# Two projections as seven block products each, and the last norm along token rows

## The reference, cut to what matters

```python
# S5 mixer: h is 512 tokens x 1024, w_in is 1024 x 4096, u takes the first 2048 columns
u_l, g_l = jnp.split(h_lat @ w_in, 2, axis=-1)
u_c, g_c = jnp.split(h_ctx @ w_in, 2, axis=-1)
...
# end of the second block: 256 tokens, 2816 -> 1024
h = h + (jax.nn.silu(gate) * val) @ w_down
return rmsnorm(h, final_norm_g)      # h * rsqrt(mean(h*h) + eps) * g, along the 1024
```

## Time and profile before

| what | value |
|---|---|
| median of 3 runs | 1619.56 us (1618.23 to 1621.71) |
| the profiled execution | 1622.5 us |
| its span, first to last instruction | 1620.7 us |
| mean granted TensorE clock | 0.979 of full speed |
| TensorE busy | 1512.4 us, 93% of the span |
| VectorE, ScalarE, GpSimd busy | 850.1, 388.6, 492.7 us |

### The profile page before, as it was taken

One profiled execution on the slowest core, in us unless ns is written; L12 is line 12 of the kernel. 1 busy time (PEld: TensorE's weight loads), 2 busy tenths in 40 slices (PEclk: granted clock), 3 DMA queues, 4 the chain that ended last, 5 costly groups with the idle time before them and its releaser, 6 DMA issues.

```text
span 1620.7 us, 25958 instructions
## 1 busy us (share of the span) xinstructions
PE 1512.4 (93%) x10248; PEld 1145.9 (71%) x10248; DVE 850.1 (52%) x1538; ACT 388.6 (24%) x889; POOL 492.7 (30%) x478
## 2 busy tenths in 40 slices
PE   5999989998999889998777999999999899999898
PEld 3444556665644478877666788888887788888787
DVE  6769265676569853367658665542441233433201
ACT  1133333333300031245444210000211011233201
POOL 0159999999894069221111000000000000000000
PEclk9999999999999999999998999999999999999999
DMA  9598787778798636669998725342443333444341
GB/s 395 161 280 270 197 209 190 185 208 199 182 276 293 251 78 189 272 213 331 324 313 258 302 107 207 142 170 105 155 146 114 105 129 108 152 155 155 123 143 72
DMA packets 70932, 318.76 MB, mean 197 GB/s; under 512 B 15536, under 2 KB 19760, under 8 KB 46256
## 3 DMA queue, kind: packets, MB, share of 16 engines
q1 hardware_dynamic: 36608, 222.84, 38.5%
q0 software_dynamic: 26672, 67.55, 17.1%
q10 hardware_dynamic: 7552, 26.96, 4.5%
HBM read 267.08 MB, written 50.20 MB: 196 GB/s over the span
## 4 chain that ended last, share of the span: by engine, by line
PE 42%; DMA 10%; DVE 1%; POOL 1%; issue 1%; ACT 1%; SPq 0%; ACTq 0%; POOLq 0%; DVEq 0%
PE bank L873 27%; PE bank L1192 10%; DMA s_responses<-arena 8%; PE bank L1310 2%; DMA arena<-in_glu 1%; POOL arena L2790 1%; DMA arena<-s_responses 1%; PE bank L1368 0%; PE bank L1355 0%; PE bank L1334 0%; DVE arena L2328 0%; PE bank L1299 0%; PE bank L1201 0%; PE bank L1147 0%; PE bank L1262 0%
## 5 line engine op out<-in xcount | busy, mean ns | idle before, releaser
L873 PE MATMUL bank<-arena,ring 128*128 128x256 f32 x1312 | 287.1, 381 | 4.4 <-DVE arena L2637 4.4
L873 PEld LDWEIGHTS bank<-arena,ring 128*128 128x128 f32 x1312 | 251.0, 191 | 39.5 <-DVE arena L2637 4.8
L873 PE MATMUL bank<-gate,ring 128*128 128x256 f32 (+1 forms) x640 | 196.7, 470 | 5.4 <-DVE gate L2532 3.4
L873 PEld LDWEIGHTS bank<-gate,ring 128*128 128x128 f32 x640 | 123.4, 193 | 78.1 <-issue 62.2
L873 PE MATMUL bank<-ht,ring 128*128 128x256 f32 (+1 forms) x544 | 175.1, 481 | 0.1
L873 PEld LDWEIGHTS bank<-ht,ring 128*128 128x128 f32 x544 | 102.5, 190 | 69.8 <-issue 60.6
L1192 PE MATMUL bank<-arena 128*128 128x256 f32 x576 | 127.3, 379 | 2.8 <-DVE pw L2372 2.5
L1192 PEld LDWEIGHTS bank<-arena 128*128 128x128 f32 x576 | 108.7, 190 | 17.9 <-issue 2.8
L1068 PE MATMUL bank<-ring,ht 128*128 128x256 f32 x512 | 114.3, 385 | 6.5 <-DVE ht L1927 6.5
L1068 PEld LDWEIGHTS bank<-ring,ht 128*128 128x128 f32 x512 | 98.4, 193 | 20.4 <-issue 6.8
L2265 DVE COPY arena<-bank 64x256 f32<-64x256 f32 x64 | 27.0, 422 | 81.8 <-PE bank L1079 80.0
(11 more groups left out here) (423 smaller groups left out, 2497.4 us busy)
## 6 DMA issues: line engine op xcount, KB each, us to landing
ring<-in_w_up SPq DMA_DIRECT2D x22, 1024.0 KB, 4.7
ring<-in_mod_tail SPq DMA_DIRECT2D x16, 1024.0 KB, 6.7
arena<-s_b_powers SPq DMA_DIRECT2D x16, 1024.0 KB, 9.4
ring<-in_glu SPq DMA_DIRECT2D x16, 1024.0 KB, 8.2
arena<-in_glu SPq DMA_DIRECT2D x16, 1024.0 KB, 9.0
arena<-s_b_rows POOLq DMA_DIRECT2D x24, 512.0 KB, 10.6
arena<-s_power_rows POOLq DMA_DIRECT2D x24, 512.0 KB, 11.4
s_b_powers<-arena POOLq DMA_DIRECT2D x24, 512.0 KB, 4.7
```

The source lines that it names most:

```text
L873: mm = pe.matmul(psum[2 * (u % 2) + m][:, 0:mv.free_size()], ring[:, sl, k, m * P:(m + 1) * P], mv, start=(kg == 0 and k == 0), stop=(kg = ...
```

## The change

```diff
-            sp.wait_ge(bm_stored, 32 * 2)
-            for b in range(2):
-                load_bm(b)
             sp.wait_ge(bm_stored, 32 * N_POOL)
             sp.wait_ge(cp_stored, 32 * N_POOL)
-            for b in range(3):
-                load_cp(b)
+            load_cp(0)
+            load_cp(2)
+            sp.wait_ge(prod_read, u_step(2, "c21"))
+            load_cp(1)
             for s in range(2):
                 load_gate(s)
+            sp.wait_ge(prod_done, u_product(3, "p6"))
+            load_bm(0)
+            sp.wait_ge(prod_done, u_product(3, "p7"))
+            load_bm(1)
+            sp.wait_ge(bbd_set, 1)
+            load_b(2)
...
-            stream("w_down", 3, 4, last=KF - 16)
...
+            sp.wait_ge(o2_done, XH)
+            for j in range(2):
+                load_down(0, j)
...
+            for j in range(2, 4):
+                load_down(0, j)
+            sp.dma_start(gain_row, a["final_norm_g_2"].partition_broadcast(P)).then_inc(x_in, 16)
+            sp.wait_ge(prod_done, down_product(0, "p1"))
+            for j in range(2):
+                load_down(1, j)
+            sp.wait_ge(sums_set, down_sum("t1"))
+            load_down(1, 2)
+            sp.wait_ge(prod_done, down_product(0, "p3"))
+            sp.wait_ge(sums_set, down_sum("t2"))
+            load_down(1, 3)
...
-                        mm = pe.matmul(psum[2 * (u % 2) + 1 - s4 // 2][:, (1 - s4 % 2) * S:(2 - s4 % 2) * S],
-                                       ht[:, k, s4 * P:(s4 + 1) * P], ring[:, sl, k, :], start=(k == 0), stop=(k == KD - 1))
-                mm.then_inc(slot_done, 1)
...
+            def u_block(c, name, bank, lhs, rhs, first=True, last=True, ready=None):
...
+                        mm = pe.matmul(psum[bank][:, (1 - t) * S:(2 - t) * S], lhs[:, k, t * P:(t + 1) * P], rhs[:, k, :],
+                                       start=(first and t == 0 and k == 0), stop=(last and k == 3), skip_group_check=True)
+                mm.then_inc(prod_done, 1)
...
+                b11, t1, b21, b22 = u_blocks(c)
...
+                    u_block(c, "p1", 0, ht[:, 0:4, lat_1], b11, ready=turned_in)
+                    u_block(c, "p2", 3, ht[:, 4:8, lat_1], b21, ready=lambda k: turned_in(4 + k))
...
+                    u_block(c, "p1", 0, ht[:, 0:4, lat_1], b11, last=False)
+                    pe.wait_ge(prod_done, u_product(c - 1, "p4"))
+                    pe.sem_inc(slot_done, 2)
...
+                pe.wait_ge(sums_set, max(u_sum("s1"), u_sum("t1", c)))
+                u_block(c, "p5", 1, s1, t1, last=False)
+                pe.wait_ge(sums_set, max(u_sum("s2"), u_sum("t2", c)))
+                if c:
+                    pe.wait_ge(prod_read, u_step(c - 1, "u3"))
+                u_block(c, "p6", 2, s2, u_t24, last=False)
+                pe.wait_ge(*u_loaded(c, 1))
+                pe.wait_ge(sums_set, u_sum("s4"))
+                pe.wait_ge(utok_set, u_copy(c, "s5"))
+                u_block(c, "p3", 1, s4, b22, first=False)
+                pe.wait_ge(sums_set, max(u_sum("s3"), u_sum("t3", c)))
+                pe.wait_ge(prod_read, u_step(c, "s2"))
+                u_block(c, "p7", 2, s3, u_t3, first=False)
+                if c == 3:
+                    responses(0)
+                if c:
+                    pe.wait_ge(utok_set, u_copy(c, "s1"))
+                    u_block(c, "p2", 0, ht[:, 4:8, lat_1], b21, first=False)
+                if c == 3:
+                    responses(1)
+                u_columns(2 * c)
+                pe.wait_ge(sums_set, u_sum("t4", c))
+                pe.wait_ge(prod_read, u_step(0, "c11") if c == 0 else u_step(c - 1, "c21"))
+                u_block(c, "p4", 3, ht[:, 4:8, lat_2], u_t24)
...
+            pe.sem_inc(slot_done, 2)
+            u_columns(7)
             pe.sem_inc(yt_set, 1)
             for q in range(2):
                 pe.wait_ge(unit_free[q], unit_at["s5_out"])
             gate_rows(0)
...
-            pe.wait_ge(ff_set, KF + 2)
-            linear("w_down", 3, 4, lambda k: ff[:, k, :], last=KF - 16)
-            for f in range(2):
-                pe.wait_ge(xn_set, 3 * KD + 4 * (f + 1))
-                for t in range(2):
-                    for j in range(4):
-                        mm = pe.transpose(psum[4 + 2 * t + f][:, j * P:(j + 1) * P], xn[:, 4 * f + j, t * P:(t + 1) * P], ident)
-                    mm.then_inc(t2_done, 1)
...
+            for h in range(2):
+                for k in range(KD):
+                    mm = pe.transpose(psum[4 + 2 * h + k // 4][:, k % 4 * P:(k % 4 + 1) * P], xl[:, k, h * P:(h + 1) * P], ident)
+                mm.then_inc(t2_done, 1)
...
+                    if ready:
+                        pe.wait_ge(ff_set, ready + k)
+                    mm = pe.matmul(psum[bank][:, 0:MT2], lhs[:, k, :], rhs(k), start=(first and k == 0), stop=(last and k == KH - 1),
...
+                if c == 0:
+                    for m in range(4):
+                        pe.wait_ge(unit_free[m // 2], unit_at["end"])
+                    down_block(0, f11, b11, ready=3)
+                    pe.wait_ge(down_in[1], 32)
+                    down_block(3, f12, b21, ready=3 + KH)
...
+                pe.wait_ge(sums_set, max(down_sum("s1"), down_sum("t1", c)))
+                down_block(1, s1, t1, last=False)
+                pe.wait_ge(sums_set, max(down_sum("s2"), down_sum("t2", c)))
...
+                down_block(2, s2, t24, last=False)
...
+                pe.wait_ge(sums_set, down_sum("t4", c))
+                pe.wait_ge(prod_read, down_step(0, "c11") if c == 0 else down_step(0, "c21"))
+                down_block(3, f22, t24)
...
+                act.wait_ge(prod_done, u_product(c, "p1"))
+                if c == 3:
+                    act.wait_ge(bm_stored, 32 * N_POOL)
+                    act.wait_ge(cp_stored, 32 * N_POOL)
+                elif c:
+                    act.wait_ge(prod_read, u_step(c - 1, "c21"))
+                act.copy(s1, psum[0][:, :]).then_inc(utok_set, 1)
+                act.wait_ge(prod_done, u_product(c, "p5"))
+                if c:
+                    act.wait_ge(prod_read, u_step(c - 1, "c22"))
+                act.copy(u_s5, psum[1][:, :]).then_inc(utok_set, 1)
...
+            for h in range(2):
+                act.wait_ge(t2_done, NB5 + 1 + h)
+                for z in range(2):
+                    act.copy(x_tok[:, h, z * 512:(z + 1) * 512], psum[4 + 2 * h + z][:, :]).then_inc(xr_set, 1)
...
+                    act.wait_ge(sq_done, 3 * KD + 2)
+                    square(0, 0, 1024, 0)
+                    act.wait_ge(sq_done, 3 * KD + 3)
+                    act.activation(r_tok[:, 0:1], row_ms[:, 0, 0:1], ACT.Sqrt, bias=eps, scale=1.0 / D).then_inc(root_set, 1)
...
+                    act.wait_ge(prod_read, down_step(1, "c21"))
+                    square(1, 512, 768, 2)
+                    act.wait_ge(sq_done, 3 * KD + 4)
+                    act.wait_ge(kv2_set, 16 + 2)
+                    act.activation(r_tok[:, 1:2], row_ms[:, 1, 2:3], ACT.Sqrt, bias=row_ms[:, 1, 0:1], scale=1.0 / D).then_inc(root_set, 1)
+                    act.wait_ge(root_set, 15)
+                    act.activation(orow[:, 1, 0:512], orow[:, 1, 0:512], ACT.Copy, scale=r_tok[:, 1:2]).then_inc(av_set, 1)
...
+            def operand(o, x, y, op, needs=0):
...
+                tt(o, x, y, op).then_inc(sums_set, 1)
...
+            u_t3_t1(0)
+            u_t2(0)
             dve.wait_ge(mod_set, 5)
...
+                else:
+                    u_columns(2 * c - 1)
+                dve.wait_ge(prod_done, u_product(c, "p6"))
+                dve.wait_ge(utok_set, u_copy(c, "s1"))
+                if c:
+                    dve.wait_ge(prod_read, u_step(c - 1, "c12"))
+                u_read(t2_, bank[2], t1_, ALU.add)
+                u_t4(c)
+                if c == 0:
+                    for k in range(4, KD):
...
+                u_read(of_unit(0, 1), by_group(bank[1]), by_group(t2_), ALU.add, u_step(c, "s2"))
...
+                u_read(t1_, bank[2], t1_, ALU.add)
...
+                u_read(of_unit(0, 0), by_group(t1_), by_group(u_s5), ALU.add, u_step(c, "u3"))
+                if c < 3:
+                    u_t3_t1(c + 1)
+                u_columns(2 * c)
+                dve.wait_ge(prod_done, u_product(c, "p4"))
...
+                u_read(of_unit(1, 0), by_group(t1_), by_group(bank[3]), ALU.subtract)
+                if c < 3:
+                    u_t2(c + 1)
+                if c < 2:
+                    for b in (2 * c, 2 * c + 1):
+                        angles(N_TURN + b)
+            u_columns(7)
...
-            add_out("w_down", 3, 3, "final_norm_g_2")
...
+            down_t3_t1(0)
+            dve.wait_ge(ff_set, KF + 2)
+            row_operand(s1, f21, f22, ALU.add)
+            row_operand(s2, s1, f11, ALU.subtract, (down_sum("s1"),))
+            down_t2(0)
+            row_operand(s4, f12, s2, ALU.subtract, (down_sum("s2"),))
+            row_operand(s3, f11, f21, ALU.subtract)
...
```

(10 more changed lines are left out.)

493 lines of the change are left out of this document (358 added, 135 removed).

## The result

The changed kernel takes 1613.23 us (median of 17 runs, 1607.41 to 1623.09) against 1621.71 us for the kernel before (17 runs, 1614.32 to 1638.17): ratio 0.995, 95% interval 0.9931 to 0.997. It is faster, by 8 us of the 23.5 that were forecast, and the time lies above the range of 1589 to 1605. The profiled execution took 1616.82 us, its span is 1615.0.

What follows compares the result with a forecast made beforehand. TensorE, busy 93% of the span, was taken to bound the kernel outside a transfer-paced loop. S5's -7 us at `inputs(0)` and the end's -16.5 us gave 1619.6 - 23.5 = 1596 us, range 1589 to 1605.

Steps and rivals of the forecast that it cites:

- The end: Last projection and final norm: start, products, waits and tail together were to give -16.5 us.
- The start: Last projection: turning the residual at once lets its first product start at 1530.6 instead of 1532.52, -1.9 us.
- The products: Last projection: 154 products at full clock take 66.5 us against 78.4 before, -11.9 us.
- The wait ahead of p5: Last projection: TensorE waits for VectorE's sums before p5, +1.5 us.
- The tail: From the last product to the end of the span: 5.5 us instead of 9.7, -4.2 us.
- The loop and all behind it: Recurrence's loop of response stores behind the S5 part: paced by transfers, carried over unchanged.
- S5, products: S5 projection: 256 block products become 224 at 0.432 us each, -13.8 us.
- S5, start: S5 projection: three sums of weights in VectorE's row before the first reciprocal delay the first product, +2.4 us.
- S5, the price of a row beside GpSimd: S5 projection: a VectorE sum of 1024 pays 1.07 us for GpSimd's operation, so it takes 2.2 us.
- S5, the waits: TensorE waiting for VectorE in S5: 2.4, 3.3 and 1 us in chunks 0 to 2, rounded down to +6.
- S5, the clock: Rival: the clock falls at every new wait, up to 14 falls of 2.4 us, giving 1630 us; chance 0.04.
- The second rival: S5 gives nothing: sums take 2.9 us by ratio (12 us of waits) or tables land late; 1602.5 us, chance 0.25.

Runs made afterwards that it cites:

- e1: Changed kernel with the S5 projection, its order on VectorE and ScalarE and its loads as before, so the end's change alone; 1610.48 us, ratio 0.9899 to before.
- e7: e5 with the latent scalings moved to chunk 3 and chunk 0's three sums of weights moved behind the sum s1; 1596.93 us, ratio 0.9854 to before.
- e8: Changed kernel without GpSimd's arithmetic for its last two of twelve tables, their transfers kept; 1599.85 us, ratio 0.9857 to before.
- e2: Changed kernel with w_down, the final norm and their loads as before, so the S5 change alone; 1627.89 us, ratio 1.003 to before.
- e5: Changed kernel with one set of angles in each chunk and ScalarE's third-diagonal copy ahead of its wait for the last read; 1599.09 us, ratio 0.9855 to before.
- e3: Changed kernel with the four sets of angles spread one, one, two over chunks 0, 1 and 2; 1599.53 us, ratio 0.9863 to before.
- e4: Changed kernel with 8 more products, which nothing reads, ahead of the wait for p7 in chunks 1 and 2; 1609.73 us, ratio 0.9907 to before.
- e11: e7 unchanged, measured again; ratio 0.9878 to before.

## Why the prediction was wrong

**The end: right, term by term.** -16.5 was forecast, -16.9 measured in the table's column (90.8 to 73.9) and 16 by e1. The start: the turned residual begins at 1539.12, p1 at 1542.00, 2.9 us behind where 2.5 was said. The products: the granted clock is 1.0 as claimed, and from p1's start to the end of the last product it is 67.7 us, 68.0 forecast. The wait ahead of p5 was 0.73 and not 1.5. The tail 5.3, not 5.5. One reading was off without effect: 1528.1 to 1530.6 is 2.5 us, not less than the 2.46 of the row. Measured, TensorE ran nothing but the 16 transposes in the 2.9 us ahead of p1, and the clock stood at 1.0.

**The loop and all behind it: right.** 182.8 against 183.6, carried over unchanged; 638.1 against 637.3 behind it.

**S5, products: right.** One block starts 3.46 us behind another, so 28 of them take 13.8 us less than 32.

**S5, start: right.** +2.4 forecast; from the centring to the first product 21.40 us after, 18.72 before, +2.7. e7 puts the price at 2.9, the means of the profiles at 2.8.

**S5, the price of a row beside GpSimd: right.** 2.2 us for a sum of 1024, measured 2.18 to 2.31 on average. Addition and not ratio, as the rival's 2.9 had it. e8 shows the cause.

**S5, the waits: the sum of the walk, not its prices.** The walk gave 2.4 (chunk 0), 3.3 (chunk 1) and 2.2 (chunk 2); measured were 2.9 (1.81 and 1.08), 3.30 and 4.00. Two steps failed. I took the 2.2 of chunk 2 down to 1 "less what falls into GpSimd's pauses" and the total down to 6: there was no such discount. And a set of angles was the middle of two ends, 3.6; it takes 4.2, near its upper end. From the first read behind p7 of chunk 1 (644.23) to the last one ahead of p7 of chunk 2 (669.83 + 0.69) VectorE's row took 26.3 us, 24.8 in the walk. With 4.2 a set and no discount the walk would have said 2.4 + 4.5 + 3.4 = 10.3, and 10.2 is what those four places measure together. The sum fits better than its parts (2.9, 3.3 and 4.0), and that is in part luck: the 1.08 ahead of the second columns, which the walk doesn't have, is cover for the next wait. The second read behind p7 of chunk 0, priced at 1.75, took 0.69 after, in a pause of GpSimd, and 1.33 in e2 to e5.

**S5, ScalarE: a wait not seen.** 1.97 us ahead of the third responses. ScalarE's row now has a wait for the last read of a product ahead of the copy of the third diagonal. I had walked TensorE against VectorE only; in e5, with the copy first, it is 1.0, and then ScalarE waits for the load of the diagonal's data (`s_b_scaled`).

**S5, the clock: priced nowhere in the sum.** 3.06 + 1.76 = 4.8 us. I had this mechanism as a rival with a chance of 0.04, because it needed ten falls to turn the sign, and took the row at 923 as proof that a wait of 2.46 us costs nothing. But I had forecast a wait of 3.3, of which that row says nothing, and its price of 2.4 stood in the text: at least one fall belonged in the likeliest sum. Nor would a row with a longer wait have settled it: e5 has one of 3.13 us with no fall, at a place where e7's clock fell behind 1.96.

Together: forecast from the first product to `inputs(0)` -9.3, measured +1.4 (129.23 to 130.63). The difference of 10.7 is 4.2 of waits for VectorE (10.2 for 6), 2.0 of ScalarE's, 4.8 of clock, and 0.3 to the other side. That 0.3 holds a term that the forecast left out: the stage starts at the low clock in both kernels, and this cost some 2.5 us before and 1.5 after, 1.0 in favour of the change; the rest goes the other way, 0.2 us for each wait in which the last product ahead of it runs out. The second rival, which had 12 us of waits, came nearest to the S5 part, for a wrong reason, the ratio; with the clock's 4.8 it would have said 1607.

**The reference point.** The prediction set 1620.7 against one profile whose centring starts at 561.04. The profile after has 568.09, and the table shows that this step is drawn anew in each execution from 558 to 570. The median of before, too, is 1621.7 in 17 runs and was 1619.6 in the three at hand. Of the 17.8 us between forecast and profile (1597.2 to 1615.0) 7.05 are this draw. Taken out, the two profiles differ by 5.7 + 7.05 = 12.8 us; the medians differ by 8.5, with 5 to 11 in the interval. Where within the executions the rest lies, one profile of each can't tell.

## What to carry to other kernels

A scheme that turns products into sums is a race between two rows of instructions. Walk both to the end and take the walk's own result, without a discount for luck. Charge a wait twice: for its length, and for the clock that may fall in it. A row with a longer wait and no fall doesn't take the second charge away (3.13 us without in e5, 1.96 with in e7). Then look which work of the late engine nobody there waits for: moving four sets of angles (e3, e5) brought more than the S5 part's whole change had cost.

Read one boundary ahead of the change in both profiles. If it has moved by as much as the effect, the difference of the spans is no measurement of the change, and stretches behind that boundary are.

## What the runs showed of the hardware

The length of a wait alone doesn't say whether the granted clock falls. It fell behind waits of 1.96 (e7), 1.97 (e2, e3, e4), 2.13 (e3), 2.62 (e2), 3.43 (e3), 3.30 and 4.00 us (after), and did not behind 1.97 (after, e8), 2.46 (before), 3.08 (e4) and 3.13 us (e5: 3.62 for p4 behind it). The 1.96, 2.62, 3.08, 3.13 and 3.43 are the same place of the program, and so are those of 1.97. A fall cost TensorE 1.5 to 3.1 us, but the path less where VectorE is late at the next step anyway (0.1 us between e7 and e11). Filling two waits with products that nobody reads kept the clock up there, and the two stretches became 4.6 us shorter (e4).

An operation of VectorE on SBUF tiles pays for the instruction that GpSimd has in hand: about 1.0 us on a sum of 1024 beside rows of 1.3 us, 0.73 on a scaling of 256 (1.14 for 0.41), and 4 us on one of 512 beside a row of 5.37, of which the first 3.5 us held it. GpSimd's operation pays up to 0.86 in turn (2.14 for 1.28).
